# Attention tiles spread later over four heads' preparation: plan share 0.84 to 0.81 in a fused encoder block

## What is computed

```python
h = rms_norm(x, pre_mix_norm)
fq, fk, fv, ff, gq, gk, gv, gb, ga, gz = split(h @ w_in)
# attention with a forget gate, 8 heads x 64, blocks of 128 queries over the causal keys
logits = q @ k.T * scale + cum[q] - cum[k]          # masked
fox_o  = rms_norm(softmax(logits) @ v)
# gated DeltaNet, 4 heads x 128: per chunk the inverse of a triangular matrix,
# then a scan over the chunks that carries a 128 x 128 state
v_new  = u - w @ state
o      = q_dec @ state + a_intra @ v_new
state  = state * g_last + k_dec.T @ v_new
x = x + rms_norm(concat(fox_o, gdn_o) @ w_out)
x = x + rms_norm(relu(rms_norm(x) @ w_up)**2 @ w_down)
```

## Time and profile before

| | us |
|---|---|
| median of 3 runs | 1482.02 |
| the runs | 1477.36 to 1483.75 |
| the profiled execution | 1477.69 |
| its span, first to last instruction | 1475.9 |
| PE busy in the span | 1380.9 (94%) |
| DVE, ACT, POOL busy | 945.8, 662.2, 636.4 |

### The profile page before, as it was taken

The page is one execution under the profiler, slowest core; times in us unless marked ns, Lnnn a source line. Parts: engine busy times, 40 slices in busy tenths (PEclk is TensorE's granted clock), DMA queues, the critical chain, the costliest instruction groups (busy, mean ns, idle before and its releaser), DMA issues.

```text
span 1475.9 us, 20694 instructions
## 1 busy us (share of the span) xinstructions
PE 1380.9 (94%) x7373; PEld 1166.7 (79%) x7373; DVE 945.8 (64%) x1498; ACT 662.2 (45%) x1406; POOL 636.4 (43%) x518
## 2 busy tenths in 40 slices
PE   6999999988889899898799979999999999999997
PEld 4778888877878798788688768888888788888885
DVE  6977777755567666665635699665555585444557
ACT  6654334445455554545633442333332344445453
POOL 3742332226365372643601468656654264442001
PEclk9999999999999999999999999999999999999999
DMA  7143333344113131012422235444442995333533
GB/s 207 47 133 104 105 114 114 109 153 153 30 58 101 44 100 44 16 44 54 119 72 86 86 102 190 157 157 157 150 150 100 311 325 184 100 93 102 206 99 143
DMA packets 135326, 177.88 MB, mean 121 GB/s; under 512 B 10493, under 2 KB 82733, under 8 KB 135225
## 3 DMA queue, kind: packets, MB, share of 16 engines
q1 hardware_dynamic: 135224, 176.56, 37.2%
HBM read 124.05 MB, written 52.48 MB: 120 GB/s over the span
## 4 chain that ended last, share of the span: by engine, by line
PE 75%; DVE 11%; issue 6%; POOL 4%; ACT 2%; DMA 1%; SPq 0%; DVEq 0%; POOLq 0%; ACTq 0%
PE ps L2996 7%; PE ps L2998 7%; PE ps L2997 7%; PE ps L3009 6%; PE ps L3011 6%; PE ps L3010 6%; PE ps L2702 6%; PE ps L2653 5%; PE ps L2655 5%; PE ps L2654 5%; PE ps L2838 3%; PE ps L2948 2%; PE ps L2950 2%; PE ps L2949 2%; PE ps L2707 2%
## 5 line engine op out<-in xcount | busy, mean ns | idle before, releaser
L3009 PE MATMUL ps<-db_hi,da_hi 128*128 128x512 f32 x448 | 175.3, 391 | 3.7 <-DVE db_lo L2265 3.6
L3011 PE MATMUL ps<-db_hi,da_lo 128*128 128x512 f32 x448 | 174.3, 389 | 0.0
L3010 PE MATMUL ps<-db_lo,da_hi 128*128 128x512 f32 x448 | 174.3, 389 | 0.0
L2263 DVE TENSOR_TENSOR da_lo<-a_raw,da_hi 128x512 fp32r<-128x512 f32 x112 | 85.3, 761 | 121.0 <-ACT da_hi L1738 120.9
L1738 ACT ACTIVATE da_hi<-a_raw 128x512 fp32r<-128x512 f32 x112 | 70.7, 631 | 158.8 <-PE ps L3011 138.4
L2996 PE MATMUL ps<-bt_hi,ring_hi 128*128 128x512 f32 x320 | 127.2, 397 | 5.2 <-DVE ring_lo L2185 5.1
L2998 PE MATMUL ps<-bt_hi,ring_lo 128*128 128x512 f32 x320 | 126.1, 394 | 0.0
L2997 PE MATMUL ps<-bt_lo,ring_hi 128*128 128x512 f32 x320 | 125.5, 392 | 0.0
L2653 PE MATMUL ps<-i_bt_hi,i_ring_hi 128*128 128x512 f32 x280 | 111.0, 396 | 3.1 <-DVE i_ring_lo L1830 1.7
L2655 PE MATMUL ps<-i_bt_hi,i_ring_lo 128*128 128x512 f32 x280 | 110.3, 394 | 0.0
L2654 PE MATMUL ps<-i_bt_lo,i_ring_hi 128*128 128x512 f32 x280 | 109.9, 393 | 0.0
(11 more groups left out here) (361 smaller groups left out, 3693.0 us busy)
## 6 DMA issues: line engine op xcount, KB each, us to landing
a_raw<-act_dram SPq DMA_DIRECT2D x112, 256.0 KB, 2.6
act_dram<-s_act SPq DMA_DIRECT2D x64, 256.0 KB, 2.1
wd<-in_w_down_dram SPq DMA_DIRECT2D x15, 1024.0 KB, 7.5
act_dram<-c SPq DMA_DIRECT2D x48, 256.0 KB, 4.8
w_top<-in_w_up_dram SPq DMA_DIRECT2D x18, 512.0 KB, 4.2
w_bot<-in_w_up_dram SPq DMA_DIRECT2D x16, 512.0 KB, 5.5
i_top<-in_w_in_dram SPq DMA_DIRECT2D x14, 512.0 KB, 4.0
i_bot<-in_w_in_dram SPq DMA_DIRECT2D x14, 512.0 KB, 5.3
```

The source lines that it names most:

```text
L3009: nc.tensor.matmul(acc, da_hi[s][:, cols], db_hi[s][:, :], start=start, stop=False, skip_group_check=True)
L3010: nc.tensor.matmul(acc, da_hi[s][:, cols], db_lo[s][:, :], start=False, stop=False, skip_group_check=True)
L3011: return nc.tensor.matmul(acc, da_lo[s][:, cols], db_hi[s][:, :], start=False, stop=stop, skip_group_check=True)
```

## The change

One number of the plan: the share of the attention's weight that is spread over the four preparations is 0.81 in place of 0.84, so 0.19 in place of 0.16 of it is planned behind the last one.

```diff
 def plan_fox():
 
-    total, share = sum(fox_weight(i) for i in range(NFT)), 0.84
+    total, share = sum(fox_weight(i) for i in range(NFT)), 0.81
     starts, done = [], 0.0
```

## The result

| | kernel before | the change |
|---|---|---|
| median of 11 runs | 1480.75 us | 1487.41 us |
| the runs | 1477.36 to 1484.53 | 1484.05 to 1491.68 |
| ratio | | 1.0042, 95% interval 1.0031 to 1.0054 |
| profiled execution, span | 1477.69, 1475.9 | 1491.64, 1489.9 |
| mean granted clock | 0.987 | 0.972 |

The change makes the kernel slower by 0.42%, some 6 us. The profiled execution of the change is among its slowest, that of before among its fastest, so their spans differ by 14.0 us, and the traces show the loss larger than it is in the median.

The account below looks back on a forecast made before the run. PE was taken as the bound in every stretch. Preparations' work -3.0, tail +2.5, DVE's queue -2.1 and fourth head's start +1.0 sum to -1.6 us, so 1480.4 us as a median, range 1471 to 1489.

Parts of the forecast that it names:

- Items 1, 3 and 4: Preparations: work moved out saves 3.0 us, DVE's queue order saves 2.1, the fourth head's start costs 1.0.
- item 4: Fourth head's start: less work covers PE's wait for `qn`, costing 1.0 us.
- Item 3: DVE's queue at four places: splits and a `max` no longer right ahead of what PE awaits; saves 2.1 us.
- Item 2: Tail: the moved 3.8 us of work costs 2.5 us, since two PE stalls get cover (0.8 and 0.5).
- what I cost at nothing: Loads of attention head 4 on SP and eight weight splits on POOL, both taken to cost no time.
- Rival A: Tail: DVE held by POOL, two more collisions of 2.37 us, giving 1485.1 us; chance 0.20.
- Rival B: Head starts: PE starved twice per head, clock falls cost 10.7 us more, giving 1491.1 us; chance 0.13.
- K: Rival from the follow-up experiments, no chance given: clock falls by chance; expected a tail without falls within 2 us of before.
- C: Whole kernel: nothing comes of it, each gap's gain is lost at another; 1482.0 us; chance 0.17.
- D: Whole kernel: every item works and two clock falls go, -10.6 us, giving 1471.4 us; chance 0.16.

Follow-up runs that it names:

- the runs with fills: POOL's eight output-weight splits replaced by zero fills, loads 1 to 5 not awaiting the third head's norms: on the change 1473.38 us, on the kernel before 1476.99 us.
- e5: The kernel before with ACT's weight splits 1 to 7 planned 2.5 units earlier and nothing else moved: 1489.6 us, ratio 1.0046.
- e2: The change with weight loads 1 to 5 no longer waiting for the third head's norms: 1485.12 us, ratio 1.0012 to the kernel before.
- e1: The change itself measured once more, nothing altered: 1489.8 us, ratio 1.0053 to the kernel before.
- e12: The change with POOL's eight output-weight splits replaced by zero fills, loads still waiting for the third head's norms: 1477.79 us, ratio 0.9970 to the kernel before.
- e11: The change with each of POOL's eight weight splits cut into four, loads still waiting for the third head's norms: 1481.04 us, ratio 0.9997 to the kernel before.
- e9: The change with POOL's weight splits each cut into four and loads 1 to 5 not awaiting the third head's norms: 1479.11 us, ratio 0.9981 to the kernel before.

## Why the prediction was wrong

The range of 1471 to 1489 held the time, but the sign was wrong: -1.6 us forecast, some +6 measured.

**Items 1, 3 and 4, the preparations: right in their sum.** They gave -3.0 - 2.1 + 1.0 = -4.1 us for the moment of the last fill. Over the eight profiled executions at 0.81 it comes at 683.7 us on average (680.2 to 686.7), over the five at 0.84 at 688.1 (686.6 to 689.5): 4.4 earlier. That the two sums agree to 0.3 us is more than such averages can tell, since single executions differ by up to 6.5 us. Of the single terms two show; the others were not separated. The wait ahead of the last `XR` of the first head is 0.88 us now. The fourth head's start waits longer for `kn`, as item 4 has it, 2.74 us against 2.09 for `qn` before. (Item 3 read one row wrongly: the third key split, at 617.17, took 1.57 us and not 1.22.)

```profile
398.84 1.13 PE L2702 MATMUL ps<-r_inv,xb 128*128 128x128 f32 x8 [0.88 <-DVE r_inv L2004]
...
597.66 0.66 PE L2707 MATMUL ps<-const,c_raw_v 128*128 128x128 f32 x4 [2.74 <-DVE kn L1972]
```

**Item 2, the tail: its own two terms were right, its bounds were not.** The cover for both stalls works: the first turn of the tail and the `pv` of tile 57 wait for nothing now:

```profile
686.85 0.63 PE L2824 MATMUL ps<-const,probs 128*128 128x128 f32 x4
...
709.81 0.45 PE L2838 MATMUL ps<-v_tok,probs_t 128*128 128x64 f32 x3
```

And with both causes away the moved work costs 3.3 us of tail (the runs with fills), where I had 2.5. But my bounds were 0.8, and 4.6 "when the tail keeps its density", and the tail grew by 11.9 and 11.6 us, past the 6 us that the prediction itself named as a sign of being wrong. The density was taken at a clock of 1.00, which the tail had before and lost. The other sign, a last fill less than 2 us earlier, showed in the first execution (0.9) and not in the second (6.4).

**The failed step is in what I cost at nothing.** I named there "the eight weight splits on POOL, whose last one ended 2 us before the tail", and looked only at the end of them. Their start hangs on loads that wait for the third head's norms, and ACT stood 0.60 us for the first of these loads already in the trace of before. A wait that the trace shows at all has no slack left, and the change brought ACT to it 2.9 us earlier. That made 3.3 us of PE's idle time. The old order with ACT 2.5 units earlier (e5) is this mistake by itself, and costs 6.8 us there; in the change it is worth the 4.4 us that free loads give back. The second half of the failure is that the splits also hold norms of DVE ahead of a `max`. By the ratios the whole adds up so: -3.6 us for 0.81 against 0.84 where neither cause acts (the fills), +4.4 for the late loads, +0.4 by which the old order with free loads lies above the kernel before, +4.9 for what POOL's splits cost more at 0.81 than at 0.84 (10.4 against 5.5), together 6.1 of the 6.2 measured. The term of 4.9 comes from the fills, which also shorten POOL's queue; how much of it is the held DVE alone was not separated.

**Rival A had the mechanism of the rest and too small a price.** I gave it 0.20 and 1485.1 us, from two collisions of 2.37 us. Collisions there were (2.15, 2.11, 1.44, 1.37 and 2.70 us on DVE, the second and the last for two norms), but the tail before has five as well (1.50, 1.27, 0.95, 1.84 and 2.13). So it is not their number that makes the difference. (Of the norms of L2068, 13 by my count, the tail now has 12 in the trace.) What I did not see is that a held norm can release loads (the first; it starts them 1.8 us later), or stand ahead of a `max` (the second), and that PE's wait behind it can be paid a second time in clock. With free loads the two orders, 0.84 and 0.81, gain 5.5 and 10.4 us from the fills. The page "SBUF — State Buffer" of the Trainium skill ("Who interferes with whom") says that a DVE instruction with two SBUF inputs contends with a GpSimd instruction that reads SBUF, and not with one that only writes it. By the fills the trace agrees: at 0.84 three norms of L2069 began while a fill of 0.95 us ran, and took 0.28 us each, like the others. At 0.81 one took 0.55, beside a `q_lo` on POOL, which reads.

**Rival B had the price nearly, and the wrong place.** The clock cost 7.2 us in the tail and 2.7 behind it in the first execution, where B had 10.7; but B had it at the heads' starts, so that its size comes out is luck. At the heads' starts the two executions of the change lie on either side of the one before. The first, and then the second:

```profile
400.00:420.00 20.00, 17.12 (x118) 15.97 (x118) 14.28 (x31) 12.52 (x36) 9.31 (x9) 0.83 0.17 54
500.00:520.00 20.00, 13.10 (x88) 11.39 (x86) 14.91 (x32) 12.33 (x38) 11.72 (x11) 0.83 0.55 158
600.00:620.00 20.00, 17.05 (x114) 15.86 (x114) 10.83 (x33) 8.44 (x32) 12.15 (x14) 0.79 0.00 1
```

```profile
400.00:420.00 20.00, 15.88 (x134) 14.78 (x134) 14.94 (x33) 13.32 (x38) 11.58 (x11) 1.00 0.21 63
500.00:520.00 20.00, 14.21 (x94) 12.20 (x95) 15.96 (x36) 12.49 (x40) 11.58 (x12) 0.83 0.40 113
600.00:620.00 20.00, 16.72 (x128) 15.39 (x127) 12.30 (x33) 9.99 (x39) 14.96 (x15) 0.91 0.01 2
```

The clock takes 20 x (0.17 + 0.17 + 0.21) = 11.0 us there in the first and 20 x (0.00 + 0.17 + 0.09) = 5.2 in the second, against 7.0 before. The 5.8 us between the two, with the same program, account for the 5.5 by which their last fills differ. The wait for `kn` at some 410 us is 2.75 us long in the first and 2.77 in the second, and the clock around it is 0.83 and 1.00. So in the preparations K is right: whether a wait brings a fall there changes from one execution to the next.

**C and D.** C is refuted by the interval, and D, faster by more, did not come. With the two causes in the tail away 0.81 is ahead of 0.84, by 3.6 us with fills and by 1.8 with quarters (by the ratios; the second is within its noise). The forecast of -1.6 had that sign.

Open: why the same wait at a head's start brings a fall of the clock in one execution and none in the next, and why waits of the same length in the tail are followed by losses from 1.7 to 6.8 us.

## What to carry to other kernels

When work is moved into a stretch, follow every queue of that stretch back to what releases it, loads first: an engine that waits for a transfer for even 0.6 us has no slack, and in a strict queue everything behind it pays. Read what a stall of PE cost as its length plus the clock that is lost behind it, from slices of the same trace, do not expect the same price in another order, and check the idle time and the busy time of a stretch apart: here the loss showed as busy time. Where GpSimd and VectorE both read SBUF, try the long GpSimd instructions cut into short ones before tuning the order around them: it gave 6.7 us here on the change and nothing clear on the old order. And which of two values of such a share is the better can depend on what happens to stand behind their collisions: 0.84 is ahead with the splits whole, 0.81 with the fills.

## What the runs showed of the hardware that I had not expected

- Behind a single wait of PE of 3.06 us the granted clock was 0.50 for the next 10 us and more (e5), and behind one of 1.46 us, in a slice with PE busy for 2.54 of 4 us, it was 0.72, 0.50 and 0.50 for 12 us (e2). The price does not follow the length: behind the wait that stands behind the late load, 3.26, 3.19, 3.12, 3.06 and 1.80 us long (the change, e1, e12, e5, e11), the clock took 1.7, 1.7, 3.4, 6.8 and 5.1 us. And in stretches with as little work (1.85 of 4 us before, at 700 to 704, by its own row) it stayed at 1.00:

```profile
700.00:704.00 4.00, 1.85 (x16) 1.50 (x15) 2.88 (x8) 3.07 (x14) 3.90 (x4) 1.00 1.20 290
704.00:708.00 4.00, 3.54 (x26) 2.94 (x25) 2.02 (x7) 3.02 (x10) 3.75 (x4) 1.00 0.89 217
```

- Cutting one POOL instruction of 2.37 us into four that take 2.8 to 2.9 us together made the kernel faster, by 6.7 us on the change (1.0042 to 0.9997). A DVE instruction gets its turn between two of POOL's: in e9 the norm of 689.07 had ended at 689.58, while the four parts of POOL's split ran from 688.70 to 691.55.
